# The first transfers of a two-layer decoder kernel, in another order

## The reference

```python
inv_freq = 1.0 / (ROPE_THETA ** (jnp.arange(0, HEAD_DIM, 2, dtype=jnp.float32) / HEAD_DIM))
ang = positions.astype(jnp.float32)[..., None] * inv_freq
cos = jnp.cos(ang)[:, :, None, :]
sin = jnp.sin(ang)[:, :, None, :]
for l in range(DEPTH):
    h = rms_norm(x, norm_mix_pre[l])
    p = h @ w_in[l]
    dn_qkv, dn_z, dn_b, dn_a, p_pool, sq, sk, sv = jnp.split(p, IN_OFFSETS, axis=-1)
    y_dn = gated_deltanet(dn_qkv, dn_z, dn_b, dn_a, ...)
    y_pool = multiscale_pool(p_pool, pool_w[l], pool_scale[l])
    y_swa = swa_sink_attention(sq, sk, sv, swa_sinks[l], cos, sin)
    mix = jnp.concatenate([y_dn, y_pool, y_swa], axis=-1) @ w_out[l]
    x = x + rms_norm(mix, norm_mix_post[l])
    h = rms_norm(x, norm_ffn_pre[l])
    x = x + rms_norm(conv_glu_ffn(h, ...), norm_ffn_post[l])
```

## Time and profile before

| | us |
|---|---|
| median of three runs (2413.10 to 2414.95) | 2413.86 |
| the profiled execution | 2415.3 |
| its span | 2413.5 |
| TensorE busy in the span | 2337.1 |
| VectorE busy | 1628.2 |
| ScalarE busy | 1082.7 |

### The profile page before, as it was taken

The page is one execution under the profiler, slowest core; times in us unless marked ns, Lnnn a source line. Parts: engine busy times, 40 slices in busy tenths (PEclk is TensorE's granted clock), DMA queues, the critical chain, the costliest instruction groups (busy, mean ns, idle before and its releaser), DMA issues.

```text
span 2413.5 us, 37404 instructions
## 1 busy us (share of the span) xinstructions
PE 2337.1 (97%) x14040; PEld 2070.0 (86%) x14040; DVE 1628.2 (67%) x2305; ACT 1082.7 (45%) x1405; POOL 45.3 (2%) x55
## 2 busy tenths in 40 slices
PE   5999999999999999999989999999999999999998
PEld 5999987788888888888889999877888888888886
DVE  4676664677787778654557766546878777785555
ACT  4554343554444444444445544336444444444443
POOL 0000001000000000000000000100000000000000
PEclk9999998999999999999999999899999999999999
DMA  6534323455565656555455333235556555565553
GB/s 199 168 112 135 106 74 123 173 191 192 177 202 177 194 188 198 202 181 201 160 160 163 118 105 111 99 140 179 187 176 202 178 192 190 180 220 177 206 178 135
DMA packets 285349, 401.24 MB, mean 166 GB/s; under 512 B 8392, under 2 KB 268514, under 8 KB 269154
## 3 DMA queue, kind: packets, MB, share of 16 engines
q1 hardware_dynamic: 283008, 399.19, 49.7%
q10 hardware_dynamic: 2274, 1.12, 0.2%
HBM read 398.20 MB, written 2.10 MB: 166 GB/s over the span
## 4 chain that ended last, share of the span: by engine, by line
PE 91%; DVE 5%; DVEq 2%; DMA 1%; ACT 1%; issue 1%; POOL 0%; SPq 0%; ACTq 0%
PE ps L1373 27%; PE ps L1354 14%; PE ps L1355 14%; PE ps L1356 14%; PE ps L1379 13%; PE ps L626 4%; DMA raw<-in_w_in 1%; DVE w_lo L1044 1%; PE ps L631 1%; PE ps L684 1%; PE ps L1421 1%; PE ps L698 0%; DVEq L1241 0%; ACT w_hi L840 0%; DVE scratch L1079 0%
## 5 line engine op out<-in xcount | busy, mean ns | idle before, releaser
L840 ACT ACTIVATE w_hi<-raw 128x1024 fp32r<-128x1024 f32 x744 | 786.1, 1060 | 1065.7 <-PE ps L1379 527.1
L1044 DVE TENSOR_TENSOR w_lo<-raw,w_hi 128x1024 fp32r<-128x1024 f32 x744 | 895.4, 1222 | 497.8 <-ACT w_hi L840 491.3
L1373 PE MATMUL ps<-h_both,w_hi 128*128 128x512 f32 x2816 | 886.9, 396 | 2.1 <-DVE w_lo L1044 1.8
L1379 PEld LDWEIGHTS ps<-h_both,w_lo 128*128 128x128 f32 x2816 | 529.7, 188 | 124.7
L1379 PE MATMUL ps<-h_both,w_lo 128*128 128x256 f32 x2816 | 554.4, 278 | 0.0
L1373 PEld LDWEIGHTS ps<-h_both,w_hi 128*128 128x128 f32 x2816 | 429.7, 189 | 3.8 <-DVE w_lo L1044 2.2
L1354 PE MATMUL ps<-w_hi,h_both 128*128 128x512 f32 x960 | 376.3, 392 | 4.1 <-DVE h_both L1143 3.3
L1355 PE MATMUL ps<-w_lo,h_both 128*128 128x512 f32 x960 | 375.5, 391 | 0.0
L1356 PE MATMUL ps<-w_hi,h_both 128*128 128x512 f32 x960 | 375.4, 391 | 0.0
L1354 PE MATMUL ps<-h_both,w_hi 128*128 128x256 f32 x1216 | 354.1, 291 | 2.1 <-DVE h_both L1066 2.1
L1356 PE MATMUL ps<-h_both,w_lo 128*128 128x256 f32 x1216 | 345.5, 284 | 0.0
(11 more groups left out here) (191 smaller groups left out, 1266.1 us busy)
## 6 DMA issues: line engine op xcount, KB each, us to landing
raw<-in_ffn_w_up SPq DMA_DIRECT2D x88, 2048.0 KB, 8.0
raw<-in_ffn_w_down SPq DMA_DIRECT2D x44, 2048.0 KB, 7.9
raw<-in_w_in SPq DMA_DIRECT2D x38, 2048.0 KB, 8.2
raw<-in_w_out SPq DMA_DIRECT2D x16, 2048.0 KB, 8.0
x<-in_x SPq DMA_DIRECT2D x2, 1024.0 KB, 8.2
scratch<-in_norm_mix_post SPq DMA_DIRECT2D x2, 1024.0 KB, 9.8
scratch<-in_norm_ffn_post SPq DMA_DIRECT2D x2, 1024.0 KB, 9.9
out_x<-x SPq DMA_DIRECT2D x4, 512.0 KB, 3.1
```

The source lines that it names most:

```text
L840: act.activation(w_hi[:, s, :], raw[:, q % 2, s * 1024:(s + 1) * 1024], ACT.Copy).then_inc(hi_done, 1)
L1044: dve.tensor_tensor(w_lo[:, s, :], raw[:, q % 2, s * 1024:(s + 1) * 1024], w_hi[:, s, :].bitcast(F32), ALU.subtract).then_inc(lo_done, 1)
L1373: pe.matmul(ps[:, up_bank(q - P_UP, i), :], w_hi[:, s, c:c + P], h_both[:, k, :, :].rearrange("p a n -> p (a n)"), start=k == 0, stop=Fals ...
L1379: return pe.matmul(ps[:, up_bank(q - P_UP, i), 0:T], w_lo[:, s, c:c + P], h_hi[:, k, :], start=False, stop=True, skip_group_check=True)
```

## The change

SP's queue at the beginning now holds x in quarters (1024 of 2048 channels for 128 tokens each) and the first pair in its four parts, interleaved; each has its own semaphore or pair of them. The gate columns and the second pair follow, then the rest of the constants, the positions, the second layer's first five parameter loads and both layers' other seven, then pool_w and the third pair. ScalarE's queue keeps the identity and the first layer's first five parameter loads (norm weights, one convolution's taps, pool scale, one norm weight).

ScalarE converts a part when it has landed and works blocks 0 and 1 of h behind parts 0 and 1, the other six behind part 3. The squares of x start one block earlier and end behind block 7. The gate columns are converted behind the first pair's h. VectorE computes the angles behind the third pair's low halves and ScalarE the sines behind the third pair's high halves. TensorE turns the first layer's first parameters at the start (bank 7) and the others between the second and third pair (`late_turn`).

```diff
+            def x_half(c):
+                for t in range(TT):
+                    sp.dma_start(x[:, t, 1024 * c:1024 * (c + 1)],
+                                 a["x"][0, t * P:(t + 1) * P, 1024 * c:1024 * (c + 1)]).then_inc(sem(f"x_in{t}{c}"), 16)
+            def first_pair(s):
+                dst, src = raw_a[:, 1, 4 * s:4 * s + 4, :], w_in[0, :, 4 * s:4 * s + 4, HEAD[0][0]:HEAD[0][0] + 256]
+                if s < 3:
+                    sp.dma_start(dst, src).then_inc(sem(f"first_in{s}"), 16)
+                else:
+                    sp.dma_start(dst, src).then_inc(landed[1], 16)
...
+                if l == 0:
+                    sp.dma_start(gw[:, 0:KT * NBA].rearrange("p (k n) -> p k n", n=NBA),
+                                 w_in[0, :, :, COL_BA:COL_BA + NBA]).then_inc(sem("first_gw"), 16)
+                    form_a(l, 2, 0, w_in, HEAD[1][0])
...
+                    for d, v in param_loads(1)[0] + param_loads(0)[1] + param_loads(1)[1]:
+                        sp.dma_start(d, v).then_inc(sem("params_in"), 16)
...
-                    gate_hi(l)
-                    hi(l, 1)
-                pre_norm(l, 0, R_PRE)
+                    for s in range(3):
+                        act.wait_ge(sem(f"first_in{s}"), 16)
+                        act.activation(w_hi[:, s, :], raw[:, 1, s * 1024:(s + 1) * 1024], ACT.Copy).then_inc(hi_done, 1)
+                        if s == 0:
+                            act.wait_ge(sem("par_ready"), 1)
+                            pre_norm(l, 0, R_PRE, (0,))
+                        if s == 1:
+                            pre_norm(l, 0, R_PRE, (1,))
+                    act.wait_ge(landed[1], 16)
+                    act.activation(w_hi[:, 3, :], raw[:, 1, 3072:4096], ACT.Copy).then_inc(hi_done, 1)
+                    pre_norm(l, 0, R_PRE, range(2, 8))
+                    act.wait_ge(sem("first_gw"), 16)
+                    act.activation(gw_hi[:], gw[:], ACT.Copy).then_inc(sem("first_gw_hi"), 1)
...
+                    if l == 0 and q == 3:
+                        act.wait_ge(sem("angle_ready"), 1)
+                        act.activation(sin_t[:], scr[:, 1, 0:T], ACT.Sin).then_inc(sem("sined"), 1)
+                        act.activation(cos_t[:], scr[:, 1, 0:T], ACT.Sin, scale=0.5).then_inc(sem("sined"), 1)
...
+                    if l == 0 and i == 1:
+                        angles()
+                    if l == 0 and i == 2:
+                        turns_of()
+                        late_params()
...
+            def late_turn():
+                pe.wait_ge(sem("params_in"), LATE_PARAMS)
+                pe.transpose(ps[:, 5, 0:R_ONE], rows1[0:R_ONE, 1, :], ident[0:R_ONE, 0:R_ONE])
+                for l in range(DEPTH):
+                    for b, n in ((0, P), (1, P), (2, FROWS - 2 * P)):
+                        ins = pe.transpose(ps[:, 3 + l, b * P:b * P + n], rows2[0:n, l, b, :], ident[0:n, 0:n])
+                ins.then_inc(sem("late_turned"), 1)
```

More of the change, by code:

```diff
@@ L851, in gate_hi, with pre_norm @@
                 act.activation(gw_hi[:], gw[:], ACT.Copy).then_inc(hi_done, 4)
[L853 to L858, removed]
+            def pre_norm(l, f, col, blocks=range(8)):
+                first = f == 0 and l == 0
+                if not first:
+                    x_squares(l, f, 0, 0)
+                    x_squares(l, f, 0, 1)
+                later = {n + 1: (n // 4, n % 4) for n in range(6)} if first else {2: (0, 2), 3: (0, 3), 4: (1, 0), 5: (1, 1), 6: (1, 2), 7: (1, 3)}
+                for b in blocks:
                     act.wait_ge(sem("h_turned"), 16 * l + (8 * f + b + 1))
@@ L865, in pre_norm @@
                         x_squares(l, f, *later[b])
+                    if first and b == 7:
+                        x_squares(l, f, 1, 2)
+                        x_squares(l, f, 1, 3)
             def post_norm(l, f, hi_next):
@@ L927, in _ @@
-            act.wait_ge(sem("pad_set"), 1)
-            act.wait_ge(sem("angle_ready"), 1)
-            act.activation(sin_t[:], scr[:, 1, 0:T], ACT.Sin).then_inc(sem("sined"), 1)
-            act.activation(cos_t[:], scr[:, 1, 0:T], ACT.Sin, scale=0.5).then_inc(sem("sined"), 1)
+            act.dma_start(const[:, 0:P], a["consts"][:, 0:P]).then_inc(sem("ident_in"), 16)
+            for d, v in param_loads(0)[0]:
+                act.dma_start(d, v).then_inc(sem("first_par"), 16)
+            act.nop().then_inc(hi_done, 4)
@@ L1174, in _, with angles @@
-            dve.tensor_scalar(ang, ang, PI_IN, -PI_IN, ALU.min, ALU.max).then_inc(sem("angle_ready"), 1)
-            dve.wait_ge(sem("sined"), 2)
-            dve.tensor_scalar(sin_t[:], sin_t[:], const[:, C_SGN:C_SGN + 1], None, ALU.mult)
-            dve.tensor_tensor(cos_t[:], cos_t[:], cos_t[:], ALU.mult)
-            dve.drain()
-            dve.tensor_scalar(cos_t[:], cos_t[:], -2.0, 1.0, ALU.mult, ALU.add)
+            def angles():
+                dve.wait_ge(sem("const_in"), 16)
+                dve.wait_ge(sem("pos_in"), 16)
+                pos, ang, turns = scr[:, 2, 0:T], scr[:, 1, 0:T], scr[:, 3, 0:T]
+                dve.tensor_copy(pos, scr[:, 0, 0:T].bitcast(I32))
+                dve.drain()
+                dve.tensor_scalar(ang, pos, const[:, C_INVF:C_INVF + 1], None, ALU.mult)
+                dve.drain()
+                dve.tensor_scalar(turns, ang, 1.0 / (2 * np.pi), MAGIC, ALU.mult, ALU.add)
+                dve.drain()
+                dve.tensor_scalar(turns, turns, MAGIC, None, ALU.subtract)
+                dve.drain()
+                for part in TWO_PI:
+                    dve.scalar_tensor_tensor(ang, turns, -part, ang, ALU.mult, ALU.add)
+                    dve.drain()
+                dve.tensor_scalar(ang, ang, PI_IN, -PI_IN, ALU.min, ALU.max).then_inc(sem("angle_ready"), 1)
@@ L1181, in _ @@
             dve.wait_ge(sem("params_turned"), 1)
-            for l in range(DEPTH):
-                dve.tensor_copy(par_all[:, l, 0:R_ONE], ps[:, l, 0:R_ONE])
-                dve.tensor_copy(par_all[:, l, R_ONE:R_ALL], ps[:, 2 + l, 0:FROWS])
+            dve.tensor_copy(par_all[:, 0, 0:R_ONE], ps[:, 7, 0:R_ONE])
             dve.drain().then_inc(sem("par_ready"), 1)
```

115 lines of the change are left out of this document (62 added, 53 removed).

## The result

| | before | after |
|---|---|---|
| median of four runs, us | 2413.72 (2413.10 to 2414.95) | 2399.71 (2397.59 to 2401.02) |
| the profiled execution | 2415.3 | 2401.02 |
| its span | 2413.5 | 2399.2 |

The ratio is 0.9941, with a 95% interval of 0.9929 to 0.9953: 14.0 us faster on the medians, 14.3 us between the two spans. The forecast was 2399.4.

A forecast was written before the change was run, and what follows sets the result against it. TensorE is busy 2337.1 of 2413.5 us; its idle start waits for the first weight pair. Second pair 15.3 us earlier, less 0.8 for late transposes, wins 14.5: 2399.4 us on the median, range 2395.5 to 2405.5.

The forecast's parts named there:

- Landing of part 3: First weight pair's last part, behind x on SP's queue: lands at 15.2 us, bounds 13.9 and 17.3.
- First parameters: First small loads on ScalarE's queue: land at about 6.5 us; at the positions' rate 12, costing at most 2 us.
- From the landing to the first pair's end: ScalarE's part 3 conversion and block 2, then TensorE's matmuls and transposes: 12.7 us after landing, clock charge apart.
- The clock charge of 1.6 us: TensorE idles some 3 us in the first pair; sixteen to eighteen matmuls then cost 0.09 more each, 1.6 us.
- The first rival: TensorE's clock stays at its lower level through the rest of the first pair: +5.9 us, 2405.3; chance 0.13.
- (2): Gate columns and second pair, following part 3, land near 24 us; ScalarE wants them at 26; up to 6 late is free.
- (3): SP issues small loads from 15 to 27 us before the third pair, which lands at 35.5, wanted at 38: hidden.
- the fourth rival: SP's small-load issues delay the third pair: deadline 37, 1.0 us an issue; win gone at 1.66; chance 0.02.
- (4): Angles and sines before the fourth pair: its part 0 ready at 73.3, TensorE wants it at 73.9 or 74.7; hidden by 1.4.
- The third rival: The angles' cover is gone; the fourth pair's part 0 is late by 2 to 4 us, about 2402.5; chance 0.10.
- (5): Sign, square and late copies on VectorE before the gates, about 2.3 us: hidden, TensorE two pairs away from needing them.
- The second rival: Small loads slow the first pair's parts to 207 GB/s: part 3 lands at 19.3, total 2403.5 us; chance 0.12.

The follow-up runs named there:

- d2_again: The changed kernel unedited, run once more as the reference of a later group on one chip; 2399.13 us, ratio 0.9940.
- d_again: The changed kernel unedited, run once more on another chip beside three other variants; 2399.12 us, ratio 0.9939.
- e_onepair: Changed kernel with all of x ahead of the first pair, and that pair in one transfer with one semaphore instead of four parts; 2405.16 us, ratio 0.9965.
- g2_apart: Changed kernel plus 19 loads of 24-byte rows on SP's queue ahead of the third pair, each partition reading a different address; 2399.74 us, ratio 0.9941.
- f_smallback: Changed kernel with the 21 late small loads back on ScalarE's queue at the start, ahead of its first conversion; 2403.63 us, ratio 0.9955.
- g_sp19: Changed kernel plus 19 loads of one 24-byte row, the same for all partitions, on SP's queue ahead of the third pair; 2415.26 us, ratio 1.0007.
- a2_fill: Second run of the changed kernel with 20 empty transposes in TensorE's wait for block 2 of h; 2396.17 us, ratio 0.9927.
- b2_order: Second run of the changed kernel with ScalarE's blocks 2 and 3 ahead of its wait for part 3, x's third-quarter transposes earlier; 2395.96 us, ratio 0.9928.
- h_sp38: Changed kernel plus 38 loads of one 24-byte row, the same for all partitions, on SP's queue ahead of the third pair; 2436.92 us, ratio 1.0094.
- b_order: First run of the changed kernel with ScalarE's blocks 2 and 3 ahead of its wait for part 3, x's third-quarter transposes earlier; 2396.25 us, ratio 0.9932.
- a_fill: First run of the changed kernel with 20 empty transposes in TensorE's wait for block 2 of h; 2396.59 us, ratio 0.9937.
- c_xfirst: Changed kernel with all four quarters of x ahead of the first pair's four parts, no interleaving; 2399.92 us, ratio 0.9945.

## Why the prediction was right

The total was right to 0.3 us, and the chosen number, the second pair's begin, to 0.5 (36.01 against 35.5). The mechanism came as said. That the total agrees to 0.3 us is in part luck: the four runs spread over 3.4 us, the beginning won 0.5 us less than the 14.5 of the sum, and the spans differ by 0.3 more than the beginning accounts for. Point by point:

- **Landing of part 3.** 15.9 against 15.2, and 15.9 to 16.1 in the other traces of this order: 0.7 late, inside the bounds of 13.9 and 17.3. At 14.0 us the transfers were on my schedule: 312 GB/s for 4 us, 376 for 3 and 374 for 4 make 3.87 MB of the 4.15 (2.05 and 2.10). The last 0.28 MB fall into the stretch from 14 to 17 us at 161 GB/s, where the gate columns in rows of 48 bytes, next in the queue, pass too. By 15.25 us the last rows of the parts have moved; I had said 14.7, since I priced the end of the pair at the rate of its middle. ScalarE starts 0.7 to 0.9 us after them, where I had put 0.5. Both together are the mis-sized term, 0.7 us.
- **First parameters.** 8.1 us against 6.5, and 8.9 in d2_again. The term was mis-sized by 1.6 to 2.4 us, well on the way to the positions' 10.3 us of issue to landing that I had named as the opposite bound. It cost ScalarE 0.40 us of waiting ahead of block 0 (0.65 in d_again), for TensorE turned x only behind the parameters; but nothing in the end, since ScalarE then waited 0.80 us for part 2 and 0.71 for part 3. In d_again and d2_again the late parameters even shortened TensorE's idle time ahead of block 2.
- **From the landing to the first pair's end.** Block 2 began 1.0 us behind the landing (1.1 said), its first matmul 1.8 later (2.0), and the pair ended at 29.97 against 29.5. That is 14.1 us from the landing; 12.7 and 1.6 for the clock were said. Gate's product and rms, 6.0, came to 6.04.
- **The clock charge of 1.6 us.** Right for the profiled execution, which has the fall after an idle of 2.13 us (some 3 said); it is absent in d_again and d2_again, and their second pair begins 1.3 us earlier. Their medians are lower by 0.6 us. It is a cost of some executions, not of the kernel. The first rival, a clock that stays low, did not come: from 24 us on it is 1.00. It says that in before TensorE had idled only once after starting; that is wrong, TensorE also waited 1.44 us ahead of 24.18. The Trainium skill's page "TensorE: Matmul & The Clock Gate", section "HAM oscillation — how this bites in real kernels", from which that rival's warning came, describes a stream that starts every piece cold; no trace of this kernel shows that with four parts, and e_onepair shows that the cutting wins 5.2 us.
- **(1) Late transposes.** 0.86 against 0.8.
- **(2) Gate columns and second pair.** Right: gw is converted at 27.33 with no wait for a transfer.
- **(3) The third pair.** SP left the small loads at 26.5 (27 said); the pair was converted from 38.99 behind TensorE, in d_again from 37.76 behind the transfer, against a landing said for 35.5. 2.3 us late, hidden. The pair took 10.2 us from issue to that conversion where I had 8.2: it stood behind the last head loads. The mechanism of the deadline was right, as g2_apart shows with an issue at 36.4 and no loss. The price in the fourth rival was not: I let the queue cost what an issue costs, 0.47 us on SP (8.97 for 19). It costs what the queue takes to work the loads off, and that is 1.1 us each where all partitions read one address. The program has six such loads ahead of the third pair; 19 more and the gain is gone.
- **(4) The angles.** Called the thinnest cover, 1.4 us. The angles were ready at 54.1, TensorE ran on, and the cover was about 3: I had counted the table load of 1.28 behind the wait for the angles, and it ran at 48.64, inside that wait. The third rival did not come.
- **(5)** Right as far as the rows go: TensorE is never idle from 40 to 80 us.
- **The second rival**, small loads that slow the parts, did not come because they are not there: with them back on ScalarE's queue the time rises by 4.5 us, near the 4.1 that the rival priced, but by ScalarE's issuing. The small loads do slow the parts: from 14 to 17 us of f_smallback the weights' queue moved 0.29, 0.27 and 0.23 MB a microsecond, against the 361 GB/s of a pair alone, and the two queues moved the same number of packets in each microsecond, 253 and 253, 270 and 271, 228 and 228. The rule of the Trainium skill's page "DMA: Bandwidth & Descriptors", section "Queues, rings and completion order", that an engine takes turns between queues by the packet, agrees with these counts. In before, 207 GB/s from 17 to 20 us was read as the price of small rows; g2_apart and g_sp19 make it likely that it was the price of the head loads (`swa_sinks` and its like, issued at 14.37): from 18 to 20 us ScalarE's queue moved 136 and 91 packets a microsecond, near the 120 of g_sp19. That was not tried apart.
- **"No stage after the beginning changes."** Nearly: the spans differ by 14.3 us where the beginning accounts for 50.84 - 36.01 - 0.86 = 14.0. But a2_fill and b2_order show that later stages can move by 2 to 4 us with no edit in them, which is nearly all of what a2_fill gains and half of what b2_order gains. Had it happened here, the sum would have been right and the total 2 to 4 us off.

## What to carry to other kernels

If the first transfer is waited for, put it first, cut it where the engines behind it can begin, and move every load that is needed later behind it; here the order was worth 8 us and the cut, on top of it, 5. Then look at the order in which the converting engine waits: a block of work that stands behind a wait that it does not need cost another 1.6 us. Price a load that is put ahead of a large one by how long the queue takes over it, not by its issue, and broadcast a tiny row to many partitions late, or in a way that has been timed. b2_order, at 2395.96 us, is the best version here and beats both kernels; the filling of a2_fill is equal and was not combined with it.

## What the runs showed of the hardware

- **Reading one address from all partitions is slow.** A load of 24 bytes to each of 128 partitions took 1.14 us when all read the same bytes (478 packets in 4 us) and at most 0.4 us when they read different ones (1392 packets in 4 us). In the changed kernel itself the same is seen where the head loads pass: from 25 to 26 us 128 packets under 512 bytes, 9 GB/s, engines' share 0.08 (first line). From 27 to 28, with the 2 MB of the third pair issued behind them at 26.5, it is still only 12 GB/s (second line):

```profile
DMA packets 140, 0.01 MB, mean 9 GB/s; under 512 B 128, under 2 KB 140, under 8 KB 140
...
DMA packets 123, 0.01 MB, mean 12 GB/s; under 512 B 103, under 2 KB 123, under 8 KB 123
```

- **A table load can run ahead of the wait of the instruction behind it.** In after ACT_TABLE_LOAD ran at 48.64, and the sine behind it began at 54.19, when the angles were ready. In before the program had two waits ahead of the sine, and the one for the angles stood at the table load itself: it ran at 15.13, only when the angles were ready. So it depends on where the wait is put.
- **TensorE's fall after a short idle.** In the first pair, after idles of 2.13 us (after), 2.10 (before, ahead of 29.83) and 2.09 (g2_apart) the clock fell to its level of 1.2 GHz for some microseconds (0.57 from 20 to 24 us in g2_apart as in after); after 1.88 (g_sp19), 1.48 (h_sp38), 1.42 and 1.26 (d_again, d2_again) it did not. But the idle near 314 us, 2.15 or 2.16 us long, was followed by a fall in after, d_again, d2_again, a2_fill and b_order and by none in a_fill, b2_order and c_xfirst. The length of the idle does not decide it alone.
- **The granted clock can read 1.00 while TensorE works at half speed.** In after, two matmuls of the first part, in the chain:

```profile
13.22 0.21 PE ps L1416
13.43 0.12 PE ps L1417
```

A matmul takes 0.21 us up to 13.43 and 0.12 from there, and the record says 1.00 for all of the stretch from 10 to 14 us, shown above. In e_onepair it says 1.00 as late as from 20 to 24 us, where matmuls come at 0.21 and only 21 begin, against 37 in d_again:

```profile
20.00:24.00 4.00, 4.00 (x21) 4.00 (x20) 2.54 (x5) 4.00 (x10) 0.00 (x0) 1.00 1.08 360
```

At a program's start the duration of one matmul tells the clock, not the record.
